# A mixture-of-experts kernel: weight units cut by rows of 4 KB, and a long expert's down product begun on half of its activations

## The reference, cut to what is touched

```python
def moe_ffn(x, router_w, router_b, w_gu, b_gu, w_down, b_down):
    ...
    def run_block(args):
        tok, e = args
        hmid = xt[tok] @ w_gu[e] + b_gu[e]
        glu = jnp.minimum(hmid[:, 0::2], SWIGLU_LIMIT)
        lin = jnp.clip(hmid[:, 1::2], -SWIGLU_LIMIT, SWIGLU_LIMIT)
        act = glu * jax.nn.sigmoid(SWIGLU_ALPHA * glu) * (lin + 1.0)
        return act @ w_down[e] + b_down[e]
```

## Time and profile before

| | us |
|---|---|
| median of 3 timed runs | 3412.9 (3412.33 to 3414.72) |
| time of the profiled execution | 3408.7 |
| its span | 3406.7 |
| TensorE busy in matmuls | 2880.0 (85%) |
| VectorE busy | 1704.5 (50%) |
| ScalarE busy | 1078.7 (32%) |
| mean granted TensorE clock | 0.91 |

### The profile page before, as it was taken

One profiled execution on the slowest core, in us unless ns is written; L12 is line 12 of the kernel. 1 busy time (PEld: TensorE's weight loads), 2 busy tenths in 40 slices (PEclk: granted clock), 3 DMA queues, 4 the chain that ended last, 5 costly groups with the idle time before them and its releaser, 6 DMA issues. The chain is left out here.

```text
span 3406.7 us, 36827 instructions
## 1 busy us (share of the span) xinstructions
PE 2880.0 (85%) x13443; PEld 2068.8 (61%) x13487; DVE 1704.5 (50%) x2698; ACT 1078.7 (32%) x1592; POOL 154.2 (5%) x173
## 2 busy tenths in 40 slices
PE   6887879999997799999944358999999999999983
PEld 5656657888776588887732247455556655457541
DVE  3864464444544644444266743744446644257413
ACT  4344333222323432222152123222334433035311
POOL 0530000000000000000012002000000000000001
PEclk9997889999998899999957658999999999999996
DMA  3110213444222122222200004899999899999994
GB/s 119 55 45 25 87 70 134 173 172 163 101 77 91 42 99 99 99 87 85 89 2 0 1 5 167 327 387 388 384 342 337 299 386 356 386 362 327 389 370 175
DMA packets 289694, 622.02 MB, mean 183 GB/s; under 512 B 9603, under 2 KB 15394, under 8 KB 289090
## 3 DMA queue, kind: packets, MB, share of 16 engines
q1 hardware_dynamic: 274816, 568.96, 46.1%
q10 hardware_dynamic: 12322, 41.38, 3.1%
q0 software_dynamic: 2304, 8.39, 0.7%
HBM read 577.54 MB, written 41.16 MB: 182 GB/s over the span
## 5 line engine op out<-in xcount | busy, mean ns | idle before, releaser
L88 DVE TENSOR_TENSOR unit_low<-unit_whole,unit_high 128x4096 fp32r<-128x4096 f32 (+3 forms) x65 | 283.8, 4366 | 191.0 <-ACT unit_high L85 190.7
L85 ACT ACTIVATE unit_high<-unit_whole 128x4096 fp32r<-128x4096 f32 (+3 forms) x65 | 225.6, 3471 | 480.4 <-PE psum L631 309.8
L2896 PE MATMUL psum<-ring_slot,hT 128*64 128x512 f32 x1008 | 306.8, 609 | 10.8 <-DMA ring_slot<-in_moe_w_gu 10.8
L631 PE MATMUL psum<-high_parts,unit_high 128*128 128x512 f32 x640 | 254.2, 397 | 9.0 <-DVE low_parts L88 9.0
L631 PE MATMUL psum<-low_parts,unit_high 128*128 128x512 f32 x640 | 252.0, 394 | 0.0
L631 PE MATMUL psum<-high_parts,unit_low 128*128 128x512 f32 x640 | 251.7, 393 | 0.0
L85 ACT ACTIVATE moe_w_high<-ring_slot 128x1024 fp32r<-128x1024 f32 x208 | 205.8, 1046 | 3.8 <-PE psum L3050 2.2
L631 PE MATMUL psum<-unit_high,hidden_high 128*128 128x512 f32 x512 | 199.6, 390 | 0.0
L631 PE MATMUL psum<-unit_high,hidden_low 128*128 128x512 f32 x512 | 199.3, 389 | 0.0
L631 PE MATMUL psum<-unit_low,hidden_high 128*128 128x512 f32 x512 | 199.2, 389 | 0.0
L631 PE MATMUL psum<-unit_high,high_parts 128*128 128x512 f32 (+2 forms) x448 | 178.4, 398 | 20.9 <-DVE low_parts L88 17.0
(11 more groups left out here) (626 smaller groups left out, 5837.3 us busy)
## 6 DMA issues: line engine op xcount, KB each, us to landing
ring_slot<-in_moe_w_gu SPq DMA_DIRECT2D x102, 2048.0 KB, 18.0
unit_whole<-in_moe_w_gu SPq DMA_DIRECT2D x34, 2048.0 KB, 13.9
ring_slot<-in_moe_w_down SPq DMA_DIRECT2D x34, 2048.0 KB, 13.0
ring_last_slot<-in_moe_w_down SPq DMA_DIRECT2D x34, 2048.0 KB, 17.5
unit_whole<-in_w_up SPq DMA_DIRECT2D x16, 2048.0 KB, 7.6
unit_whole<-in_w_down SPq DMA_DIRECT2D x16, 2048.0 KB, 7.7
expert_rows<-zero_row ACTq DMA_DIRECT2D x15, 1536.0 KB, 5.3
unit_whole<-in_w_in SPq DMA_DIRECT2D x5, 2048.0 KB, 7.7
```

Of the source, the lines that this page charges most:

```text
L85: return act.activation(self.high, self.whole, ACT.Copy)
L88: return dve.tensor_tensor(self.low, self.whole, self.high.bitcast(F32), ALU.subtract)
L631: ins = pe.matmul(bank, a, c, start=(i == 0 and m == 0), stop=(i == len(products) - 1 and m == len(parts) - 1))
L2896: ins = pe.matmul(banks[g], xg[:, c, 0:HALF], w[g][:, c, :], start=(c == 0), stop=False)
```

## The change

Four things change together.

1. A unit is now 512 rows of 1024 columns, 4 KB in a row: unit 0 and 1 are the upper and the lower half of the rows of w_gu's first 1024 columns, unit 2 and 3 those of its last 1024, unit 4 and 5 those of w_down. A unit is split in four slices of 128 rows instead of four quarters of 256 rows by 512 columns. The short experts read the same numbers from the new places.
2. In a long expert two PSUM banks fill side by side: units 0 and 1 into banks 2 and 3, units 2 and 3 into 4 and 5, units 4 and 5 into 6 and 7. The biases come in pairs after units 1, 3 and 5.
3. The activations are made in two halves. The first half is turned between units 2 and 3, the second between units 4 and 5. Unit 4 needs only the first half (it holds the upper 512 rows of w_down). The first half of the gather stays ahead of unit 4, the second comes after the second turn.
4. Clips, sigmoid and products are done once for two banks (128 x 512) instead of once for each. The first expert keeps its float32 path. The semaphore that counts used quarters is also what SyncE waits for now.

The diff, cut to its core:

```diff
     def up(self, pe, j, wait_unit, xg, par):
 
         k, T = self.k, self.tables
-        for n in range(4):
-            w = wait_unit(pe, n)
-            if n >= 2:
-                pe.wait_ge(self.act_ready, 4 * j + n - 1)
-            bank = k.psum[:, 2 + n % 2, :]
-            for c in range(KT):
-                pe.matmul(bank, xg[:, c, :], w[:, c, :], start=(c == 0), stop=False)
-            pe.matmul(bank, T.bias_ones[:, par, :], T.bias_parts[:, n * 512:(n + 1) * 512], start=False, stop=True)\
-              .then_inc(self.up_full, 1)
-
-
-
+        for pair in range(2):
+            for r in range(2):
+                w = wait_unit(pe, 2 * pair + r)
+                for g in range(2):
+                    n = 2 * pair + g
+                    bank = k.psum[:, 2 + g, :]
+                    if r == 0 and pair == 1:
+                        pe.wait_ge(self.act_ready, 4 * j + n - 1)
+                    for c in range(HALF_K):
+                        pe.matmul(bank, xg[:, HALF_K * r + c, :], w[:, c, g * 512:(g + 1) * 512],
+                                  start=(r == 0 and c == 0), stop=False)
+                    if r == 1:
+                        pe.matmul(bank, T.bias_ones[:, par, :], T.bias_parts[:, n * 512:(n + 1) * 512], start=False,
+                                  stop=True).then_inc(self.up_full, 1)
...
-                    ins = pe.matmul(banks[g], xg[:, c, 0:HALF], w[g][:, c, :], start=(c == 0), stop=False)
-            if parted and pair == 1:
-                ins.then_inc(self.quarter_used.sem, PARTED)
+                    ins = pe.matmul(banks[g], xg[:, c, 0:HALF], w[c // HALF_K][:, c % HALF_K, g * 512:(g + 1) * 512],
+                                    start=(c == 0), stop=False)
+            if parted:
+                ins.then_inc(self.quarter_used.sem, 2 * HALF_K if pair else HALF_K + 1)
...
+    def unit_used(self, eng, j, n, parted=False):
+
+        if parted:
+            eng.wait_ge(self.quarter_used.sem, self.used_at(j, n, HALF_K - 1))
+        elif n < 4:
...
+    def round_quarters(self, act, j, n, loaded):
+        act.wait_ge(self.loaded[n], loaded)
+        for q in range(HALF_K):
+            if n >= 2:
+                act.wait_ge(self.quarter_used.sem, self.used_at(j, n - 1, q))
+            elif self.waits_from(j, 2):
+                act.wait_ge(self.quarter_used.sem, self.used_at(j - 1, 5, q))
+            self.quarter(n, q).round(act).then_inc(self.k.unit_rounded.sem, 1)
...
+    def unit_products(self, pe, j, n, banks, a, first, a_low_at=None):
+        for q in range(HALF_K):
+            w, f = self.quarter(n, q), HALF_K * (n % 2) + q
+            pe.wait_ge(self.k.unit_split.sem, self.split_at(j, n, q))
+            for g in range(2):
+                cols = slice(g * 512, (g + 1) * 512)
+                pe.matmul(banks[g], a.high[:, f, :], w.high[:, cols], start=(first and q == 0), stop=False)
+                pe.matmul(banks[g], a.high[:, f, :], w.low[:, cols], start=False, stop=False)
+            if q == 0 and a_low_at is not None:
                 pe.wait_ge(self.k.unit_split.sem, a_low_at)
-            for c in range(2):
-                ins = pe.matmul(bank, stationary[:, 2 * q + c, :], moving[:, c, :], start=(first and i == 0 and c == 0),
-                                stop=False)
+            for g in range(2):
+                ins = pe.matmul(banks[g], a.low[:, f, :], w.high[:, g * 512:(g + 1) * 512], start=False, stop=False)
+            ins.then_inc(self.quarter_used.sem, 1)
+
+    def turn_act_pair(self, pe, j, pair):
+        k, T = self.k, self.tables
+        pe.wait_ge(self.act_ready, 4 * j + 2 * pair + 2)
+        for i in range(HALF_K):
+            f = HALF_K * pair + i
+            ins = pe.transpose(k.psum[:, 2 + pair, i * P:(i + 1) * P], T.act[:, f * P:(f + 1) * P], k.ident[:, :])
+        ins.then_inc(self.act_turned, 1)
+
+    def banks(self, first):
+        return [self.k.psum[:, first + g, :] for g in range(2)]
+
+    def biases(self, pe, banks, parts, at, par, full):
+        for g in range(2):
+            pe.matmul(banks[g], self.tables.bias_ones[:, par, :], parts[:, (at + g) * 512:(at + g + 1) * 512], start=False,
+                      stop=True).then_inc(full, 1)
+
+    def up_parted(self, pe, j, wait_unit, xg, par):
+        T = self.tables
+        early, late = self.banks(2), self.banks(4)
+        w = wait_unit(pe, 0)
+        for g in range(2):
+            for c in range(HALF_K):
+                ins = pe.matmul(early[g], xg[:, c, :], w[:, c, g * 512:(g + 1) * 512], start=(c == 0), stop=False)
         ins.then_inc(self.quarter_used.sem, 1)
-
-    def up_parted(self, pe, j, wait_unit, xg, par):
+        self.unit_products(pe, j, 1, early, T.xg_parts, False)
+        self.biases(pe, early, T.bias_parts, 0, par, self.up_full)
+        self.unit_products(pe, j, 2, late, T.xg_parts, True)
+        self.turn_act_pair(pe, j, 0)
+        self.unit_products(pe, j, 3, late, T.xg_parts, False)
+        self.biases(pe, late, T.bias_parts, 2, par, self.up_full)
...
+    def down_and_turn_parted(self, pe, j):
+        pe.wait_ge(self.actT_ready, 2 * j + 1)
+        pe.wait_ge(self.o_whole, 2 * j)
+        self.unit_products(pe, j, 4, self.banks(6), self.tables.act_parts, True, self.act_low_at(j, 0))
+        self.turn_act_pair(pe, j, 1)
+
+    def down_parted(self, pe, j, par):
+        pe.wait_ge(self.actT_ready, 2 * j + 2)
+        self.unit_products(pe, j, 5, self.banks(6), self.tables.act_parts, False, self.act_low_at(j, 1))
+        self.biases(pe, self.banks(6), self.tables.down_parts, 0, par, self.down_full)
...
+        def clip(pair):
+            dve.wait_ge(self.up_full, 4 * j + 2 * pair + 2)
+            dve.wait_ge(self.act_ready, 4 * j + 2 * pair)
+            both = k.psum[:, 2 + 2 * pair:4 + 2 * pair, :].rearrange("p b (f two) -> p b f two", two=2)
+            dve.tensor_scalar(T.glu[:, :, :], both[:, :, :, 0], 7.0, None, ALU.min).then_inc(self.glu_ready, 2)
+            dve.tensor_scalar(T.lin[:, :, :], both[:, :, :, 1], 7.0, -7.0, ALU.min, ALU.max).then_inc(self.lin_ready, 2)
+
+        def multiply(pair):
+            q = 4 * j + 2 * pair + 2
+            dve.wait_ge(self.gate_ready, q)
+            dve.wait_ge(self.lin_ready, q)
+            dve.scalar_tensor_tensor(out=T.lin[:, :, :], in0=T.lin[:, :, :], scalar=1.0, in1=T.sig[:, :, :], op0=ALU.add,
+                                     op1=ALU.mult).then_inc(self.prod_ready, 2)
+            dve.wait_ge(self.prod_ready, q)
+            if pair == 0:
+                dve.wait_ge(self.down_full, 2 * j)
+            dve.tensor_tensor(T.act[:, pair * 512:(pair + 1) * 512], T.lin[:, :, :].rearrange("p b f -> p (b f)"),
+                              T.glu[:, :, :].rearrange("p b f -> p (b f)"), ALU.mult).then_inc(self.act_ready, 2)
+
+        def split_act(pair):
+            dve.wait_ge(self.actT_ready, 2 * j + pair + 1)
+            dve.tensor_tensor(self.act_tiles(T.act_parts.low, pair), k.psum[:, 2 + pair, :],
+                              self.act_tiles(T.act_parts.high, pair).bitcast(F32), ALU.subtract)\
                .then_inc(k.unit_split.sem, 1)
-            for i in range(QUARTERS):
-                self.split_quarter(dve, j, 5, i)
+
+        self.split_xg(dve, j, xg)
+        for q in range(HALF_K):
+            self.split_quarter(dve, j, 1, q)
+        for pair in range(2):
+            n = 2 + 2 * pair
+            for q in range(HALF_K - 1):
+                self.split_quarter(dve, j, n, q)
+            clip(pair)
+            self.split_quarter(dve, j, n, HALF_K - 1)
+            multiply(pair)
+            for q in range(HALF_K):
+                self.split_quarter(dve, j, n + 1, q)
+            split_act(pair)
...
+        self.round_quarters(act, j, 1, loaded)
+        for pair in range(2):
+            self.round_quarters(act, j, 2 + 2 * pair, loaded)
+            act.wait_ge(self.glu_ready, 4 * j + 2 * pair + 2)
+            act.activation(T.sig[:, :, :], T.glu[:, :, :], ACT.Sigmoid, scale=1.702).then_inc(self.gate_ready, 2)
+            self.round_quarters(act, j, 3 + 2 * pair, loaded)
+            act.wait_ge(self.act_turned, 2 * j + pair + 1)
+            act.activation(self.act_tiles(T.act_parts.high, pair), k.psum[:, 2 + pair, :], ACT.Copy)\
+               .then_inc(self.actT_ready, 1)
...
+    rows = slice(n % 2 * HALF_K * P, (n % 2 + 1) * HALF_K * P)
     if n < 4:
-        w = k.ins["moe_w_gu_2"][0][bass.ds(e, 1), :, n * 512:(n + 1) * 512]
+        w = k.ins["moe_w_gu_2"][0][bass.ds(e, 1), rows, n // 2 * 1024:(n // 2 + 1) * 1024]
     else:
-        w = k.ins["moe_w_down_2"][0][bass.ds(e, 1), :, (n - 4) * 512:(n - 3) * 512]
+        w = k.ins["moe_w_down_2"][0][bass.ds(e, 1), rows, :]
...
-                    E.turn_act(pe, j)
+                    if parted:
+                        E.down_and_turn_parted(pe, j)
+                    else:
+                        E.turn_act(pe, j)
                 if ahead:
```

(39 more changed lines are left out.)

130 lines of the change are left out of this document (36 added, 94 removed).

## The result

The changed kernel took 3350.0 us (median of 4 runs, 3347.7 to 3354.1) against 3412.6 for the kernel before: ratio 0.982, interval 0.980 to 0.983. On a second chip it gave 3354.1 (5 runs) beside 3409.1, ratio 0.984 (0.9825 to 0.985). So the gain is 55 to 63 us, and the forecast of 41 us, 3372 with a range that reached down to 3358, was too small. The kernel before gave 3400 to 3416 over all of its runs, so that 8 us of the difference between 55 and 63 is the spread between executions.

The account below looks back on a forecast made before the run. In the experts' stage TensorE and the loads were both taken as 94% used. Terms for waits, clock, biases and loads summed to -41.3 us, 3412.9 to 3371.6, say 3372; range 3358 to 3395.

Parts of the forecast that it names:

- copies: Long experts: TensorE's waits for the copied (turned) activations go, -1.1 us.
- The turn: Long experts: unit 4 covers the second turn, so its waits of 26.5 us go; first turn's wait taken as 0.
- the last expert's 1.7: Last long expert, no gather to cover unit 5: 1.3 us open plus 0.4 for the low part, +1.7.
- Start of a long expert, +3.0: Unit 1 cannot start earlier and its bias matmul (0.23 us) now comes after it: 13 x 0.23 = +3.0 us.
- Parts of weights, -1.7: Long experts: waits for parts of weights go, as unit 2 then comes behind two biases, -1.7 us.
- the five waits behind jumps: Waits marked issue ahead of experts that begin a new round of the loop of four: the change does nothing to them.
- The clock, -13.6: Seven low-clock stretches behind the turn's waits in 13 long experts go, -13.6 us; bound on the other side 0.
- The loads, -3.1: Weight loads, 4 KB rows for 2 KB: rate +2.4% (bounds 0 and 5%), counted as 5.0 - 4.0 + 1.4 + 0.7 us.
- rival B: 4 KB rows bring nothing and load waits replace the turn's: 7.1 lost plus 6 us, 3385; chance 0.15.
- Rival D: Wider rows help more; no short expert waits for loads, 13.5 us and low clock behind go: -55, 3358; chance 0.08.

Follow-up runs that it names:

- shifted pair: Kernel before and changed kernel, each with one unused memset of about 1 us ahead of the experts' stage: 3411.6 (ratio 1.0004) and 3356.1 (0.985).
- The late turn: Changed kernel with the second turn, its copy and low part put back ahead of unit 4, rows still 4 KB: 3405.1, ratio 0.998.
- Filling the turns' waits: Kernel before with six unused 512-column matmuls ahead of the turn's wait in each long expert: 3403.1 beside 3410.0, ratio 0.998.
- without jumps: Kernel before with its loop of rounds written out: 3376.4 beside 3409.1, ratio 0.991.
- the table: Changed kernel, new order or late turn; one transfer 4 KB, two 4 KB, two 2 KB: ratios 0.982/0.984, 0.986, 0.993; late 0.998, 1.001, 1.0045.

## Why the prediction was wrong, step by step

Against the profiled pair, in the window of the result (a forecast part, what it measured, and the same from the two kernels shifted by a microsecond):

| | forecast | measured | shifted pair |
|---|---|---|---|
| TensorE's waits: turn, parts, copies, last expert, loads, and those behind jumps | -30.7 | -26.7 | -35.0 |
| low clock | -13.6 | -23.0 | -14.6 |
| bias handovers and the rest of TensorE's work | +3.0 | about -5 | about -5 |
| sum | -41.3 | -54.5 | -54.6 |

The waits are the sums of all entries of the lists (70.6 us before, 43.9 after; shifted 76.9 and 41.9). The clock is half of the time in which TensorE was at work at the low level (72.8 and 26.8 us; shifted 52.9 and 23.8). The last line is what remains. Of the 13 us that the forecast missed, 8 are in the last term in both pairs. The other 5 are in waits and clock together, 44.3 forecast and 49.7 measured in either pair; which of the two gets them differs from one pair to the other.

The turn. Right. No wait is left at either turn, and none at unit 3 or unit 5 of the 12 clean long experts. The last long expert has 1.2 + 1.2 us (L3070, L3075) for the 1.7 forecast. The late turn puts the price of the step, with its clock, at 51 to 53 us against the 38 that the forecast had for it (26.5 + 13.6 less the last expert's 1.7), but from waits of 2.7 us, not 2.0.

Start of a long expert, +3.0. This is the step that failed: the term was mis-sized, and wrong in sign. What stands in its place is about -5 us, 0.4 us less in each long expert where 0.23 more was forecast. Unit 1 starts 6.98 us after unit 0 where it took 7.10, where the forecast held it to the old time. The two biases behind unit 1 then cost little: unit 2 begins 5.97 us after unit 1 (2423.93 to 2429.90). A unit with no bias behind it takes 5.80 us (2429.90 to 2435.70), and one with a single bias took 5.84 where TensorE did not wait:

```profile
2478.75 0.82 PE L3050 MATMUL psum<-moe_w_high,moe_xg_high 128*128 128x512 f32 x2
...
2484.59 0.83 PE L3050 MATMUL psum<-moe_w_high,moe_xg_high 128*128 128x512 f32 x2
```

The two turns of four take 0.35 us each for the 0.85 of eight. From the expert's start to unit 2 it is 12.95 us (2416.95 to 2429.90), where the forecast's own terms give 7.10 + 5.71 + 2 x 0.23 = 13.27. A clean expert came to 41.1 for 41.8.

Parts of weights, -1.7. Right in clean experts, but 6.3 us stand behind three jumps. The forecast said that the change does nothing to the five waits behind jumps. They went from 18.2 to 15.9 us, and what followed them changed too: the lateness that a low clock had covered came into view.

The clock, -13.6. It counted the stretches behind turns, and those behave as said (27.2 us to none at a turn; 3.4 stand at unit 5 of the last long expert). It left the 30.6 us behind jumps as a constant; they fell to 6.8 in the profiled execution and to 10.2 in the second chip's. Holding them constant was the lesser fault of the forecast, and what the profiled pair shows of it, -23.0, is too large: the shifted kernel before has 17.0 us behind its jumps without any change, and at the three jumps into long experts the faster unit 0 ran into a wait. Why the changed kernel has less low clock behind its jumps stays open. Filling the turns' waits does not do it (27.2 us are left), and with the late turn and its longer waits there are 17.0. The reverse influence is seen: without jumps, two stretches behind turns are left of seven.

The loads, -3.1. In the sum this term came out near: the waits for loads went from 13.5 to 11.1 us, in the shifted pair from 14.2 to 10.2. The steady rate was taken as +2.4% with 5% as bound; it is 403 for 386, +4.4%, and in the windows of the last expert 411 for 391. A larger fault, though none of the missing 13 us, is what the rate was multiplied with. The forecast priced wider rows by the waits that the kernel before had. Their worth lies in the waits that the faster TensorE would have had without them: 22 us by the table, of which the forecast had 7.1 + 6 in its rival B. That rival, the new order with no gain from rows, was put at 3385; the kernel with 2 KB rows took 3385.9, though some 10 us of it are its second transfer. Seen from the sum, the rows kept the load waits at 15.2 where 25.1 had come, both with two transfers, which no line of a profile after shows as a gain. Rival D (no waits for loads at all) did not happen.

The range failed by the same two steps: its low end, 3358, was rival D's alone, and no rival had TensorE's own work in a long expert become shorter or the experts behind jumps change.

## What to carry to other kernels

Where two resources are both near full, price an edit to the second by what it is worth after the first has become faster: here 4 KB rows gave 11 us with the late turn and 22 with the new order, a difference just clear of noise. Price low clock and waits together: two profiles of the kernel before, one of them shifted by a microsecond, differ by 20 us at the low level and hardly in time. Do not split a gain by a single pair of profiles; a shifted copy of each kernel shows which parts of the split hold. A change of order can also change what the same matmuls take, so give that term a bound on the other side of zero. And look behind every jump of a loop when loads saturate the DMA engines: here five jumps cost 25 to 33 us, more than the rows.

## What the hardware showed beyond that

- A jump back cost each engine a wait of its own while the loads ran at 386 to 403 GB/s: TensorE 2.6 to 4.4 us in the kernels before and after, and 5.0 us on average with 24 more matmuls in the body. Where the program moves on from the last of the 32 experts to `extra_blocks`, VectorE was held 15 to 18 us, and 24.5 and 21.6 us in the two kernels with two transfers of 2 KB rows.
- One transfer of 2 MB against two of 1 MB, the same rows and bytes: the two took some 6 to 10 us longer, with the steady rate unchanged (402 to 404 GB/s). The Trainium skill, in "Perfetto Trace Analysis", section DMA Optimizations, says that splitting transfers may let some of them start sooner, and the whole task end sooner if the DMA engines are generally idle; here, full as they are, nothing was gained by it.
- Bias matmuls behind a unit are nearly free: a unit took 5.80 us with none, 5.84 with one and 5.97 with two.
